# A hybrid decoder trunk on one core: VectorE multiplies four tiles before it adds them, and reads each group's first tile one list earlier

## The reference, cut to what matters

```python
for l in range(2):
    xn = rms_norm(x, norm_mix[l])
    h = xn @ w_in[l]                    # q, k, v of two attentions, low-rank c_q and c_kv, gates
    ... three attentions: o_a, o_b, o_c, each (512, 512)
    branches = jnp.stack([o_a, o_b, o_c], axis=2)
    proj = jnp.einsum('bsgc,gcd->bsgd', branches, w_branch[l])
    gates = jax.nn.sigmoid(hg.reshape(b, s_len, N_BRANCHES, d))
    x = x + jnp.sum(gates * proj, axis=2) @ w_out[l]
    x = x + hierarchical_moe(rms_norm(x, norm_ffn[l]), ...)
```

## Time and profile before

| | |
|---|---|
| median of 3 runs | 1525.47 us (1524.52 to 1525.71) |
| the profiled execution | 1524.72 us |
| its span, first to last instruction | 1522.6 us |
| PE busy | 1468.6 us, 96% of the span |
| DVE busy | 925.8 us, 61% |
| ACT busy | 860.9 us, 57% |
| POOL busy | 397.5 us, 26% |
| mean granted TensorE clock | 0.988 |
| share of PE in the chain that ended last | 83% |

### The profile page before, as it was taken

The page is one execution under the profiler, slowest core; times in us unless marked ns, Lnnn a source line. Parts: engine busy times, 40 slices in busy tenths (PEclk is TensorE's granted clock), DMA queues, the critical chain, the costliest instruction groups (busy, mean ns, idle before and its releaser), DMA issues.

```text
span 1522.6 us, 22440 instructions
## 1 busy us (share of the span) xinstructions
PE 1468.6 (96%) x7894; PEld 1142.2 (75%) x7894; DVE 925.8 (61%) x1806; ACT 860.9 (57%) x1660; POOL 397.5 (26%) x554
## 2 busy tenths in 40 slices
PE   8999999999999999999899999999999999999994
PEld 6887777677777787777678867776677777877773
DVE  3555655544554447999854566645445544489996
ACT  5446656655453335888644655565554433468883
POOL 3414227520000013453105053195000000225211
PEclk9999999999999999999999999999999999999997
DMA  7722222142232357999876321222422323769996
GB/s 187 137 76 64 63 60 68 55 117 60 67 97 84 115 185 240 351 364 349 292 192 115 80 63 53 67 70 56 106 67 63 111 84 105 246 224 370 370 360 238
DMA packets 155384, 231.06 MB, mean 152 GB/s; under 512 B 20579, under 2 KB 89955, under 8 KB 155268
## 3 DMA queue, kind: packets, MB, share of 16 engines
q1 hardware_dynamic: 143780, 209.62, 45.6%
q0 software_dynamic: 10768, 17.80, 3.5%
q10 hardware_dynamic: 720, 2.16, 0.4%
HBM read 220.99 MB, written 29.69 MB: 165 GB/s over the span
## 4 chain that ended last, share of the span: by engine, by line
PE 83%; DVE 8%; ACT 3%; issue 2%; DMA 2%; ACTq 0%; SPq 0%; POOLq 0%; DVEq 0%
PE bank L545 22%; PE bank L547 20%; PE bank L546 20%; PE bank L1673 4%; PE bank L1658 3%; PE bank L1649 3%; PE bank L1651 3%; DVE xT L617 2%; PE bank L648 2%; ACT xT L611 2%; DVE gate_t L2094 1%; PE bank L1705 1%; DMA q_c<-ytok 1%; PE bank L1708 1%; PE bank L1644 1%
## 5 line engine op out<-in xcount | busy, mean ns | idle before, releaser
L545 PE MATMUL bank<-wh,xT 128*128 128x512 f32 (+1 forms) x960 | 399.3, 416 | 6.5 <-DVE gate_t L2094 4.7
L547 PE MATMUL bank<-wh,xT 128*128 128x512 f32 (+1 forms) x960 | 374.1, 390 | 0.0
L546 PE MATMUL bank<-wl,xT 128*128 128x512 f32 (+1 forms) x960 | 373.3, 389 | 0.0
L486 ACT ACTIVATE wh<-raw,gcol 128x512 fp32r<-128x512 f32 (+1 forms) x208 | 149.0, 717 | 204.6 <-PE bank L547 204.6
L493 DVE SCALAR_TENSOR_TENSOR wl<-raw,gcol,wh 128x512 fp32r<-128x512 f32 (+1 forms) x208 | 161.4, 777 | 135.5 <-ACT wh L486 128.5
L545 PEld LDWEIGHTS bank<-wh,xT 128*128 128x128 f32 x960 | 180.8, 188 | 73.3 <-issue 23.0
L547 PEld LDWEIGHTS bank<-wh,xT 128*128 128x128 f32 x960 | 180.4, 188 | 37.5
L546 PEld LDWEIGHTS bank<-wl,xT 128*128 128x128 f32 x960 | 181.3, 189 | 29.8 <-issue 1.4
L2032 DVE CUSTOM_DVE_ANT_0 prob<-bank,mask 128x128 f32<-128x128 f32 (+3 forms) x128 | 60.5, 490 | 190.0 <-PE bank L1649 100.9
L1820 ACT ACTIVATE prob<-prob,nmax 128x128 f32<-128x128 f32 (+3 forms) x192 | 107.4, 561 | 113.2 <-DVE nmax L2032 112.9
L2336 POOL TENSOR_TENSOR rows<-x_rows,ac 128x512 f32<-128x512 f32 x16 | 22.2, 1404 | 502.8 <-DVE x_rows L2103 502.8
(11 more groups left out here) (334 smaller groups left out, 2711.9 us busy)
## 6 DMA issues: line engine op xcount, KB each, us to landing
raw<-in_w_in_dram SPq DMA_DIRECT2D x192, 256.0 KB, 2.7
bqkv<-in_w_expert_gate_dram SPq DMA_DIRECT2D x64, 256.0 KB, 5.6
bqkv<-in_w_expert_up_dram SPq DMA_DIRECT2D x64, 256.0 KB, 7.8
bqkv<-in_w_expert_down_dram SPq DMA_DIRECT2D x32, 512.0 KB, 8.5
q_c<-in_w_expert_gate_dram SPq DMA_DIRECT2D x64, 256.0 KB, 5.8
q_c<-in_w_expert_up_dram SPq DMA_DIRECT2D x64, 256.0 KB, 8.2
head_odd<-in_w_expert_down_dram SPq DMA_DIRECT2D x32, 512.0 KB, 8.8
raw<-in_w_branch_dram SPq DMA_DIRECT2D x48, 256.0 KB, 2.6
```

What stands on the lines that cost most here:

```text
L486: nc.scalar.activation(wh[:, i % HL, 0:width], raw[:, i % RAW, 0:width], ACT.Copy, scale=piece_gain(i))\
L545: nc.tensor.matmul(out, lhs[0], rhs[0], start=start, stop=False)
L546: nc.tensor.matmul(out, lhs[0], rhs[1], start=False, stop=False)
L547: return nc.tensor.matmul(out, lhs[1], rhs[0], start=False, stop=stop)
```

## The change

In `read_group` the additions of `branch` 2 to 5 are taken out. They stand in a function `merge`, called in `after_read` behind the wait for each tile, so that DVE does the four products first and then, tile by tile, an addition, a wait for that addition and the signal `branch_ready`. For `branch` 5, whose sums are read ahead of slot 134, the four products and then the four additions stand in a row, with no wait between the additions. `read_ahead(s)` is true for the last slot of every group but gates, up to slot 132: there `read_group(g, 0)` is called in the list of slot s itself, behind `split_lo(s + 2)` and ahead of `scale`; the list of slot s + 1 then starts with tile 1.

```diff
                         nc.vector.scalar_tensor_tensor(out=gate_t[:, n, :], in0=gate_t[:, n, :], scalar=1.0,
                                                        in1=src, op0=ALU.add, op1=ALU.mult).then_inc(acc_read, 1)
-                        sums_read(dve, g, n)
-                        nc.vector.tensor_tensor(rows[:, n, cs], rows[:, n, cs], gate_t[:, n, :], ALU.add)\
-                            .then_inc(merged, 1)
...
+            def merge(idx, n):
+                cs = slice(512 * (idx % 2), 512 * (idx % 2 + 1))
+                nc.vector.tensor_tensor(rows[:, n, cs], rows[:, n, cs], gate_t[:, n, :], ALU.add).then_inc(merged, 1)
+
             def after_read(g, n):
...
+                sums_read(dve, g, n)
                 if name == "branch" and idx >= 2:
+                    merge(idx, n)
                     dve.wait_ge(merged, of(merged, 4 * (idx - 2) + n + 1))
-                sums_read(dve, g, n)
...
+            def read_ahead(s):
+                g = PIECES[s][0]
+                return END[g] == s and s + 1 < OUT0 and GROUPS[g][0] != "gate"
...
                     if s == OUT0:
                         for n in range(NT):
                             read_group(PIECES[s - 1][0], n)
+                        for n in range(NT):
+                            sums_read(dve, PIECES[s - 1][0], n)
+                            merge(GROUPS[PIECES[s - 1][0]][1], n)
                         dve.wait_ge(merged, of(merged, 16))
...
                     if ended:
-                        read_group(g, 0)
+                        if not read_ahead(s - 1):
+                            read_group(g, 0)
                         read_group(g, 1)
...
+                    if read_ahead(s):
+                        read_group(PIECES[s][0], 0)
                     for p in pair:
                         scale(p)
```

More of the change, by code:

```diff
@@ L2092, in read_group @@
                     else:
-                        m = 4 * (idx - 2) + n
                         nc.vector.scalar_tensor_tensor(out=gate_t[:, n, :], in0=gate_t[:, n, :], scalar=1.0,
                                                        in1=src, op0=ALU.add, op1=ALU.mult).then_inc(acc_read, 1)
-                        sums_read(dve, g, n)
-                        nc.vector.tensor_tensor(rows[:, n, cs], rows[:, n, cs], gate_t[:, n, :], ALU.add)\
-                            .then_inc(merged, 1)
                 else:
```

## The result

| | before | changed |
|---|---|---|
| median of 22 executions each | 1523.8 us (1521.3 to 1526.5) | 1527.0 us (1523.0 to 1530.5) |
| the profiled execution | 1524.72 us | 1522.98 us |
| its span | 1522.6 us | 1521.0 us |

The ratio is 1.0019, with a 95% interval of 1.0014 to 1.0025: the change makes the kernel slower by some 3 us. The forecast was -0.4 us. One thing is odd and is the key to this case: the profiled execution of the changed kernel is the fastest of its 22, and by its trace nothing is lost at all.

The account below looks back on a forecast made before the run. PE, busy for 96% of the span, was taken to bound the kernel; terms of -3.37 + 3.32 - 0.46 + 0.29 = -0.2 us a layer, -0.4 in both, gave a median of 1525.1 us, range 1522.4 to 1528.4 us.

Parts of the forecast that it names:

- Slots 122 and 134: Branch 4 and 5, no attention left: four products back to back return both slots to 2.72 us, gaining 3.37 us a layer.
- Slots 98 to 111: Additions ahead of the split and divisions delay PE's turns in slots 99 and 111 by 1.66 us each, 3.32 a layer.
- The step between additions: Time from one DVE addition's start to the next in slots 98 and 110, taken as 0.83 us, between 0.72 and 0.95.
- The rival by which the additions would follow at 0.61 us: DVE's additions follow each other without a cost of waiting: -2.6 us, so 1522.4 us; chance 0.09.
- The vanishing stop of tile 3: PE's stop at tile 3 before the turn goes, about 0.42 us, but PE then waits about 2.1 us at the turn.
- The 14 early reads that move past nothing: In 14 of 16 slots reading tile 0 one list earlier leaves DVE's instruction order the same, so nothing changes.
- Slots 68 to 73: Early reads in slots 68 and 72: 0.29 us lost at slot 69, 0.46 us gained at slot 73, in a layer.
- The weights that they hold up are wanted two slots later; I cost that at nothing: After slots 122 and 134, additions end about where they did before, so the weights behind them cost PE nothing.
- The prediction's own test for a cost: Held-up weights would cost if the additions ended later than the start of slot 124 minus one split of 0.75 us.
- The choice of the likeliest case: Whole kernel: the forecast of 1525.1 us, with its own range 1523 to 1527.4 us, was given chance 0.67.
- The third rival: PE's clock falls in stops before turns of slots 99 and 111, 1.64 us each; chance 0.12 for one or two, 0.07 more.
- The sum without the clock: Whole kernel: -3.37 + 3.32 - 0.46 + 0.29 = -0.2 us in a layer, -0.4 us in both layers.

## Why the prediction was right or wrong

**Slots 122 and 134: right**, 1.75 and 1.61 us against 1.76 and 1.61.

**Slots 98 to 111: right in size.** The step between additions was the unknown; 0.83 was taken and 0.84 measured. With the other measured terms that is 0.60 + 3 x 0.84 + 0.69 + 0.23 = 4.04 instead of 4.05 us, and each place lost 1.64 instead of 1.66 us. The rival by which the additions would follow at 0.61 us falls. The changed kernel has the comparison itself: in slot 134 the four additions stand in a row, and none waits for the addition before it,

```profile
527.26 2.49 DVE L2103 TENSOR_TENSOR rows<-rows,gate_t 128x512 f32<-128x512 f32 x4
```

with a step of (2.49 - 0.69) / 3 = 0.60 us. So the wait and the signal between two additions cost 0.24 us.

**The vanishing stop of tile 3: right**, and right that it is lost again in the wait before the turn. It gave 0.58 and 0.66 us, more than the 0.42 that was read off.

**The 14 early reads that move past nothing: right**; no such slot changed.

**Slots 68 to 73: right in sign.** ACT was not what tile 0 of slot 73 waited for: it now starts at 280.01, right behind the transpose, and tile 1 stops for DVE's read, as was said. The terms were off by 0.1 and 0.25: slot 69 lost 0.38 instead of 0.29, slots 71 to 73 gained 0.71 instead of 0.46. Together -0.33 instead of -0.17.

```profile
279.65 0.60 PE L1708 MATMUL bank<-ident,head_odd 128*96 128x128 f32 x4
280.01 0.48 PE L545 MATMUL bank<-wh,cT_kv 128*128 128x512 f32 x1
281.29 0.50 PE L545 MATMUL bank<-wh,cT_kv 128*128 128x512 f32 x1 [0.33 <-DVE rows L2090]
```

**"The weights that they hold up are wanted two slots later; I cost that at nothing": wrong.** PE waits for the split in slot 124:

```profile
492.37 3.20 DVE L2103 TENSOR_TENSOR rows<-rows,gate_t 128x512 f32<-128x512 f32 x4
496.16 2.08 DVE L493 SCALAR_TENSOR_TENSOR wl<-raw,gcol,wh 128x512 fp32r<-128x512 f32 x3 [0.58 <-DVE rows L2103]
```

```profile
496.96 0.50 PE L545 MATMUL bank<-wh,xT 128*128 128x512 f32 x1 [0.35 <-DVE wl L493]
```

"The number of operations is the same" overlooked that PE comes 1.76 us sooner. The prediction's own test for a cost would not have shown it: the additions end at 492.37 + 3.20 = 495.57, and slot 124 was due at 493.74 + 2.72 = 496.46, less one split 495.71. The test left out the time from the last addition to the split, 0.58 us here and 0.23 in layer 1. The cost is 0.61 and 0.29 us in the two layers.

**The choice of the likeliest case: wrong, and this is the step that failed.** The sum of -0.4 us was made as if PE's clock stood still. The third rival named the mechanism, the places and, to 0.1 us, the price (1.64 against 1.53), and the prediction gave a clock under 1.00 in slots 98 to 111 as a sign of being wrong. But the rival had a chance of 0.12 for one or two falls and 0.07 for more, and 0.67 went to the forecast with no fall. The argument against it, "2 us of standing between dense matmuls is little", rested on no row: the trace of before has no stop of that length in a dense part, neither with nor without a fall. Its nearest rows, stops of about 1 us between small matmuls once with and once without a fall, should have spoken for a fall now and then at twice the length, in four places. With two falls at the measured 1.53 us the forecast would have been +2.7 us; the medians differ by 3.2.

**The sum without the clock: right, in part by luck.** The slots give +0.06 us in both layers together against -0.4. Each of the large terms was right, but the gain of slots 69 to 73 was put 0.16 us a layer too small and the cost of slots 123 and 124 was left out, and these two errors partly cancel.

**Where the gain went.** 3.37 us a layer were gained where no attention is left, and 3.28 us lost where it is, because the same edit took two additions out of idle time of DVE and put all four ahead of the divisions. What tipped the balance is that the waits of 0.8 us at most became stops of over 2 us, and PE's clock sometimes fell behind these.

What stays open: how the falls are spread over the four places in the executions without a trace, why the same stop has a fall in one layer and not in the other, and the shortest stop that can cause one. Between dense matmuls 1.1 us had none in one execution and 2.1 us had some; in the router, between small matmuls, there was half clock behind stops of about 1 us.

## What to carry to other kernels

When producer work is batched to free a resource sooner, look at what stands behind the batch in the same engine's list: here the gain of 3.4 us a layer was handed back by divisions that PE waited for, and moving the additions behind those turned +3 us into -10 us. Add up stops of PE not only by their length: here each of more than 2 us also put its clock at risk, at 1.5 us a fall. A trace of the fastest execution can hide that, so compare the median of many with the sum over the trace, and look for the difference in the granted clock.

## What the runs showed of the hardware that was not expected

PE's clock fell to half behind some of its stops of 2.1 to 2.3 us between dense matmuls, in 1 of 4 places in the trace with only the additions moved, 2 of 4 in the second trace of the changed kernel, 3 of 4 with the long stops made in the kernel before, and 0 of 4 in the changed kernel's first trace. Each fall in these places lasted a little over 3 us and cost 1.5 us. Filling the stops with transposes of the identity brought the median from 1527.4 back to 1524.0 us, and the two traces with filled stops have no fall at any of the eight places.

A step from one addition on DVE to the next, with a wait for the first, a signal and a wait between them, took 0.84 us, against 0.60 for additions of the same size in a row, none of which waits for the one before.
